# The same kernel with the weights' slots at other addresses: 32 bytes more from slot to slot, and 192 more ahead of the low parts

## The chip, the cores and the metric

One core of a Trainium2 chip. The metric is the device time of one execution in microseconds; the time before is the median of three runs.

## The reference, cut to what matters

Two layers of a hybrid model (latent attention, gated delta rule, block attention side by side) and then four layers of another one, on 256 tokens of 1024 features, all in float32. Most of the arithmetic is the feed-forward block, which the last four layers hold twice each:

```python
def swiglu(x, w_gu, w_down):
    g, u = jnp.split(x @ w_gu, 2, axis=-1)
    return (jax.nn.silu(g) * u) @ w_down
```

with 1024 features in and out and 2816 inside. The other products with weights are projections into and out of the mixers (latent attention, delta rule, linear attentions, windowed attention) and a gate. All of them have the same form in the kernel.

## The kernel before

**Weights as chunks.** The host lays all weights out as 781 chunks of 128 partitions x 1024 float32 (4096 bytes in each partition). Chunk c arrives by DMA in slot c mod 4 of w_raw (load, line 80). ACT writes the high part, a copy rounded to TensorE's fp32r format, into slot c mod 6 of w_hi (hi, line 90). DVE subtracts it from the raw one and writes the low part into slot c mod 6 of w_lo (lo, line 98). The three engines work up to five chunks ahead of TensorE. TensorE reports a chunk as done (chunk_done), and then ACT may fill its slot again.

**Products.** A float32 product is made of three fp32r ones: high weights with high activations (line 138), low weights with high activations (line 139), high weights with low activations (line 144), as products (lines 146 and on) puts them in a row. In each of them 128 columns of a slot are the stationary operand, and 256 columns of activations move. Each matmul is one LDWEIGHTS and one MATMUL, and no two neighbours share both operands. rows (lines 153, 154 and 158) is the same with the roles exchanged: the slot's columns move, 256 or 512 of them, and activations are stationary.

**Order of work.** One feed-forward block (ffn, from line 415 on) takes for each of 22 tiles a gate chunk, an up chunk and the down chunk of the tile before. A gate or up chunk is 8 x 3 products into one half of a bank of ps_gu, the moving operand being xn_hi[:, j, :] and xn_lo[:, j, :], a new j for every three. A down chunk is 8 x 3 products into ps_acc, the moving operand being h_hi[:, t % 2, :] and h_lo[:, t % 2, :], the same for all eight. In the first tile of a block gate and up are made together, and the products alternate between the two halves of the bank. The small projection of p (ple) and the latents of the first two layers lie in h_hi and h_lo too. Every other product with weights moves (or, in rows, holds) xn_hi and xn_lo.

**Where the tensors lie.** setup (lines 722 and on) allocates the tensors one after another, each rounded up to 32 bytes, in every partition alike. By the compiled program of the kernel before they begin at these bytes of a partition:

| tensor | begins at | modulo 512 |
|---|---|---|
| w_raw, 4 slots of 4096 | 16,512 | 128 |
| w_hi, 6 slots of 4096 | 32,896 | 128 |
| w_lo, 6 slots of 4096 | 57,472 | 128 |
| x_res, xn | 82,048 and 90,240 | 128 |
| xn_hi (two), xn_lo (two) | 98,432 to 123,008, steps of 8192 | 128 |
| silu, h | 132,512 and 134,560 | 416 |
| h_hi, h_lo, 4 slices of 1024 each | 136,608 and 140,704 | 416 |
| ones, const | 146,176 and 154,880 | 256 |
| arena | 165,536 | 160 |

Slices of 128 columns in a chunk and the slices of xn and h are multiples of 512 bytes apart.

Of the kernel before, what the change touches and what calls it, by code (L numbers as in the profile page):

```python
# [7 lines left out]
F32R = mybir.dt.float32r  # L8
# [4 lines left out]
P = 128  # L13
# [5 lines left out]
FT = FF // P  # L19
CH = 1024  # L20
NS = 6
NR = 4
TURN = 12
STEP = 4
AHEAD = NS - 1
EPS = 1e-6
# [29 lines left out]
class Kernel:  # L56
# [19 lines left out]
    def load(self, sp, c, i=0):  # L76
        s = c % NR
        if c >= NR:
            sp.wait_ge(self.w_lo_ready.sem, c - NR + 1 + i * TURN)
        sp.dma_start(self.w_raw[:, s, :], self.w_dram[c + i * TURN, :, :]).then_inc(self.w_loaded[s].sem, 16)  # L80

    def hi(self, act, c, i=0):

        if c >= self.n_chunks:
            return
        s, r = c % NS, c % NR
        act.wait_ge(self.w_loaded[r].sem, 16 * (c // NR + 1) + i * 16 * (TURN // NR))
        if c >= NS:
            act.wait_ge(self.chunk_done.sem, c - NS + 1 + i * TURN)
        act.activation(self.w_hi[:, s, :], self.w_raw[:, r, :], ACT.Copy).then_inc(self.w_hi_ready.sem, 1)  # L90

    def lo(self, dve, c, i=0):

        if c >= self.n_chunks:
            return
        s = c % NS
        dve.wait_ge(self.w_hi_ready.sem, c + 1 + i * TURN)
        dve.tensor_tensor(self.w_lo[:, s, :], self.w_raw[:, c % NR, :], self.w_hi[:, s, :], ALU.subtract)\  # L98
           .then_inc(self.w_lo_ready.sem, 1)
# [315 lines left out]
def ffn(k):  # L415
# [27 lines left out]
    def _(pe):  # L443
        def down(t, c, i):
            pe.wait_ge(*hl.at(b0 + t + 1 + STEP * i))
            k.wait_chunk(pe, c, i)
            for m in range(KD):
                mm = k.products(pe, k.ps_acc[:, m // 2, (m % 2) * S:(m % 2 + 1) * S], c % NS, m * P, P,
                                k.h_hi[:, t % 2, :], k.h_lo[:, t % 2, :], False, t == FT - 1,
# [272 lines left out]
def setup(nc, ctx, io, n_chunks, n_vec, n_const=1):  # L722
    k = Kernel(nc, ctx, n_chunks)
    k.w_dram = io["w"]
    k.w_raw = k.sb("w_raw", [P, NR, CH])
    k.w_hi = k.sb("w_hi", [P, NS, CH], F32R)
    k.w_lo = k.sb("w_lo", [P, NS, CH], F32R)
    k.x = k.sb("x_res", [P, KD, S])
    k.xn = k.sb("xn", [P, KD, S])
    k.xh = [k.sb(f"xn_hi{b}", [P, KD, S], F32R) for b in range(2)]  # L730
    k.xl = [k.sb(f"xn_lo{b}", [P, KD, S], F32R) for b in range(2)]
    k.cur, k.read_until, k.p_read = 1, [0, 0], 0
    k.rstd = k.sb("rstd", [P, S])
    k.rcol = k.sb("rstd_columns", [P, TT])
    k.mean_sq = k.sb("mean_square_columns", [P, TT])
    k.powers = k.sb("powers", [P, 2 * TT])
    k.latent_col = k.sb("latent_columns", [P, 2 * TT])
    k.eps = k.sb("eps", [P, TT])
    k.inner_sq, k.inner_col, k.outer_col = (k.sb(n, [P, TT]) for n in ("inner_square_columns", "inner_columns", "outer_columns"))
    k.both_gains = k.sb("both_gains", [P, KD])  # L740
    k.inner = None
    k.norms = 0
    k.s = k.sb("silu", [P, 2, S])
    k.h = k.sb("h", [P, 2, S])
    k.h_hi = k.sb("h_hi", [P, 4, S], F32R)
    k.h_lo = k.sb("h_lo", [P, 4, S], F32R)
    k.lat_hi, k.lat_lo = k.h_hi[:, 0:3, :], k.h_lo[:, 0:3, :]
    k.vec = k.sb("vec", [P, n_vec])
    k.ones = k.sb("ones", [P, P])
    k.p_all = k.sb("p_all", [P, 4, 2, S])  # L750
    k.t5b = k.p_all[:, :, :, :].rearrange("p a b t -> p (a b) t").rearrange("p (q h) t -> p q h t", q=2)
    k.const = k.sb("const", [P, n_const])
    k.t5 = k.sb("t5", [33, 4])
    k.ba = k.sb("ba", [P, 16])
    k.tiny = k.sb("tiny", [P, 16])
    k.lbw = k.sb("bounds", [P, 8 * KD])
    k.arena = Arena(k.sb("arena", [P, ARENA]), ARENA)
    k.acc_by = []
    k.slot = k.side_bank = 0
    k.y_at = {}  # L760
    k.adds = None
    k.late = ((), ())
    ps = [ctx.enter_context(nc.psum_tensor(f"ps_gu{i}", [P, 2 * S], F32)) for i in range(2)]
    k.ps_gu = ps
    k.ps_acc = ctx.enter_context(nc.psum_tensor("ps_acc", [P, 4, 2 * S], F32))
    k.ps_sum = ctx.enter_context(nc.psum_tensor("ps_sum", [P, 2 * S], F32))
    k.ps_misc = ctx.enter_context(nc.psum_tensor("ps_misc", [P, 2 * S], F32))
    k.w_loaded = [k(f"w_loaded{s}") for s in range(NR)]
    k.w_hi_ready, k.w_lo_ready, k.chunk_done = k("w_hi_ready"), k("w_lo_ready"), k("chunk_done")
    k.gu_read = [k("product_read_act").made()] * 2  # L770
    k.side_read = [k("product_read_dve").made()] * 2
    k.block = ctx.enter_context(nc.Block())
    return k
# [3106 lines left out]
def build(nc, io, out, n_chunks):  # L3880
    with ExitStack() as ctx:
        k = setup(nc, ctx, io, n_chunks, N_VEC, N_CONST_1)
        k.ident = con(k, "ident")
        start(k, io)
# [89 lines left out]
```

## Time and profile before

| | |
|---|---|
| median of 3 runs | 2543.4 us (2542.41 to 2544.77) |
| span of the profiled execution | 2542.1 us; the page gives no other time of it |
| PE busy | 2497.2 us |
| DVE busy | 1729.5 us |
| ACT busy | 1322.2 us |
| DMA, mean | 165 GB/s |

The span goes from the first to the last instruction of the profiled execution, and is 1.3 us under the median of the runs. Busy times of PE are of overlapping instructions: a MATMUL of 256 columns is shown with some 285 ns, while the next starts much earlier. The distance from start to start is what one costs. The timeline gives starts to 0.01 us, so a pace is read over many products in a row.

### The profile page before, as it was taken

To read this page: it belongs to the slowest core of one execution; us is meant where nothing else is said; L and a number is where in the kernel's file an instruction comes from. 1 tells how busy PE (TensorE), PEld (TensorE's weight loads), DVE (VectorE), ACT (ScalarE), POOL (GpSimd) and SP (SyncE) were. 2 spreads that over 40 slices of the span, in tenths; PEclk is the share of its full clock that TensorE was granted. 3 is DMA by queue.
4 is the path that set the end of the run, shared out by engine and by line. 5 is a ranking of instruction groups with operands and counts; after the bars stand their busy time and mean duration, and the time that the engine had idled before them with its cause. 6 is when DMAs were issued, how large, how long until landed. Compare 5 with 4: busy or idle time off the path is not lost.

```text
span 2542.1 us, 51688 instructions
## 1 busy us (share of the span) xinstructions
PE 2497.2 (98%) x20402; PEld 2466.2 (97%) x20402; DVE 1729.5 (68%) x2416; ACT 1322.2 (52%) x2021; POOL 97.1 (4%) x99
## 2 busy tenths in 40 slices
PE   8989989999999999999999999999999999999999
PEld 7989989999999999999999999998999999999999
DVE  7768767657775576657666675587666765877556
ACT  5735735446664454445544554466445544755444
POOL 1010010000200000000000000000000000220000
PEclk9999999999999999999999999999999999999999
DMA  7314315554345555555355455543555555435553
GB/s 255 108 51 164 119 51 193 180 189 167 141 156 185 183 179 181 179 187 175 133 191 181 165 192 189 183 141 116 194 185 171 188 179 186 161 122 183 182 184 122
DMA packets 115233, 418.85 MB, mean 165 GB/s; under 512 B 12816, under 2 KB 13968, under 8 KB 114832
## 3 DMA queue, kind: packets, MB, share of 16 engines
q1 hardware_dynamic: 114240, 413.10, 47.2%
q8 instruction: 108, 1.77, 0.3%
q0 software_dynamic: 560, 2.10, 0.2%
q10 hardware_dynamic: 288, 1.57, 0.2%
q14 instruction: 37, 0.30, 0.0%
HBM read 414.62 MB, written 2.10 MB: 164 GB/s over the span
## 4 chain that ended last, share of the span: by engine, by line
PE 88%; DVE 7%; ACT 2%; issue 1%; DMA 0%; POOL 0%; SPq 0%; ACTq 0%; DVEq 0%
PE ps_gu L138 17%; PE ps_gu L144 17%; PE ps_gu L139 17%; PE ps_acc L144 8%; PE ps_acc L138 8%; PE ps_acc L139 8%; DVE w_lo L98 2%; PE ps_acc L2641 1%; DVE arena L1615 1%; ACT w_hi L90 1%; PE ps_acc L2207 1%; PE ps_sum L138 1%; PE ps_sum L366 1%; PE ps_sum L139 1%; PE ps_sum L144 1%
## 5 line engine op out<-in xcount | busy, mean ns | idle before, releaser
L98 DVE TENSOR_TENSOR w_lo<-w_raw,w_hi 128x1024 fp32r<-128x1024 f32 x781 | 953.6, 1226 | 423.2 <-ACT w_hi L90 422.7
L138 PE MATMUL ps_gu<-xn_hi,w_hi 128*128 128x256 f32 x3832 | 1084.2, 286 | 28.4 <-DVE w_lo L98 13.0
L139 PE MATMUL ps_gu<-xn_hi,w_lo 128*128 128x256 f32 x3832 | 1076.2, 284 | 0.0
L144 PE MATMUL ps_gu<-xn_lo,w_hi 128*128 128x256 f32 x3832 | 1035.9, 284 | 0.0
L90 ACT ACTIVATE w_hi<-w_raw 128x1024 fp32r<-128x1024 f32 x781 | 819.7, 1054 | 411.2 <-PE ps_gu L144 303.8
L138 PEld LDWEIGHTS ps_gu<-xn_hi,w_hi 128*128 128x128 f32 x3832 | 738.1, 193 | 33.5 <-DVE w_lo L98 13.7
L139 PEld LDWEIGHTS ps_gu<-xn_hi,w_lo 128*128 128x128 f32 x3832 | 739.0, 193 | 0.2
L144 PEld LDWEIGHTS ps_gu<-xn_lo,w_hi 128*128 128x128 f32 x3832 | 714.9, 192 | 0.0
L144 PE MATMUL ps_acc<-h_lo,w_hi 128*128 128x256 f32 x1496 | 420.4, 281 | 0.0
L138 PE MATMUL ps_acc<-h_hi,w_hi 128*128 128x256 f32 x1496 | 419.6, 280 | 0.2 <-DVE h_lo L545 0.2
L139 PE MATMUL ps_acc<-h_hi,w_lo 128*128 128x256 f32 x1496 | 416.5, 278 | 0.0
L515 ACT ACTIVATE silu<-ps_gu 128x256 f32<-128x256 f32 x176 | 67.9, 386 | 450.9 <-DVE ps_gu L536 450.9
L138 PEld LDWEIGHTS ps_acc<-h_hi,w_hi 128*128 128x128 f32 x1496 | 281.9, 188 | 0.4 <-DVE h_lo L545 0.4
L139 PEld LDWEIGHTS ps_acc<-h_hi,w_lo 128*128 128x128 f32 x1496 | 281.9, 188 | 0.0
L144 PEld LDWEIGHTS ps_acc<-h_lo,w_hi 128*128 128x128 f32 x1496 | 280.7, 188 | 0.0
L536 DVE TENSOR_TENSOR ps_gu<-ps_gu,rstd 128x512 f32<-128x512 f32 x176 | 123.1, 699 | 87.9 <-PE ps_gu L144 87.6
L540 DVE TENSOR_TENSOR h<-silu,ps_gu 128x256 f32<-128x256 f32 x176 | 74.2, 422 | 90.2 <-ACT silu L515 90.2
L138 PE MATMUL ps_acc<-xn_hi,w_hi 128*128 128x256 f32 x336 | 96.3, 290 | 0.3 <-DVE w_lo L98 0.3
L139 PE MATMUL ps_acc<-xn_hi,w_lo 128*128 128x256 f32 x336 | 93.9, 283 | 0.0
L393 POOL TENSOR_TENSOR rstd_columns<-mean_square_columns,powers 128x2 f32<-128x2 f32 x17 | 15.1, 886 | 1978.7 <-ACT mean_square_columns L379 1978.7
L144 PE MATMUL ps_acc<-xn_lo,w_hi 128*128 128x256 f32 x336 | 88.6, 283 | 0.0
L545 DVE TENSOR_TENSOR h_lo<-h,h_hi 128x256 fp32r<-128x256 f32 x176 | 73.9, 420 | 7.7 <-ACT h_hi L519 7.7
(462 smaller groups left out, 2651.3 us busy)
## 6 DMA issues: line engine op xcount, KB each, us to landing
w_raw<-in_w_dram SPq DMA_DIRECT2D x781, 512.0 KB, 3.9
const<-in_const_dram SPq DMA_DIRECT2D x1, 1280.0 KB, 12.2
x_res<-in_x_dram SPq DMA_DIRECT2D x2, 512.0 KB, 7.6
distance_rows<-arena POOLq DMA_DIRECT2D x1, 1024.0 KB, 5.8
p_all<-distance_rows POOLq DMA_DIRECT2D x2, 512.0 KB, 6.0
p_all<-in_p_dram ACTq DMA_DIRECT2D x1, 1024.0 KB, 7.7
out_dram<-x_res SPq DMA_DIRECT2D x8, 128.0 KB, 1.9
const<-in_const_dram ACTq DMA_DIRECT2D x1, 512.0 KB, 9.6
```

The costliest lines, as they stand in the source:

```text
L90: act.activation(self.w_hi[:, s, :], self.w_raw[:, r, :], ACT.Copy).then_inc(self.w_hi_ready.sem, 1)
L98: dve.tensor_tensor(self.w_lo[:, s, :], self.w_raw[:, c % NR, :], self.w_hi[:, s, :], ALU.subtract)\
L138: pe.matmul(out, self.w_hi[:, s, j0:j0 + width], rhs_hi, start=start, stop=False, skip_group_check=True)
L139: pe.matmul(out, self.w_lo[:, s, j0:j0 + width], rhs_hi, start=False, stop=False, skip_group_check=True)
L144: return pe.matmul(out, self.w_hi[:, s, j0:j0 + width], rhs_lo, start=False, stop=last, skip_group_check=True)
L366: mm = pe.matmul(k.ps_sum[:, tt:tt + 1], k.xn[:, m, tt * P:(tt + 1) * P], k.ones[:, 0:1], start=(m == 0 and tt == 0), stop=(m == tiles[-1] ...
L515: act.activation(k.s[:, t % 2, :], k.ps_gu[t % 2][:, 0:S], ACT.Silu).then_inc(silu.sem, 1)
L536: dve.tensor_tensor(gu, gu, k.rstd[:, :].unsqueeze(1).to_broadcast([P, 2, S]), ALU.mult).then_inc(sc.sem, 1)
L540: dve.tensor_tensor(k.h[:, t % 2, :], k.s[:, t % 2, :], k.ps_gu[t % 2][:, S:2 * S], ALU.mult)\
L545: dve.tensor_tensor(k.h_lo[:, t % 2, :], k.h[:, t % 2, :], k.h_hi[:, t % 2, :], ALU.subtract)\
L1615: eng.scalar_tensor_tensor(out=qkv[:, t, :], in0=raw[:, b, j:j + S], scalar=w(j), in1=qkv[:, t, :], op0=ALU.mult, op1=ALU.add).then_inc(*c ...
L2207: mm = pe.matmul(at_bank(acc01, n), four(Lm[lv % 2])[:, n, :], four(T)[:, n, :], start=(n % 4 == 0), stop=True, skip_group_check=True)
```

## The change

The slots of w_hi and of w_lo are made 1032 columns long in place of 1024; the eight columns at the end of each (32 bytes) are not used. Between the two tensors lies an unused one of 48 columns (192 bytes). Every tensor that is allocated after them moves up by 576 bytes. No instruction is added, removed or put elsewhere.

```diff
@@ -19,6 +19,7 @@
 FT = FF // P
 CH = 1024
 NS = 6
+SHIFT = 8
 NR = 4
 TURN = 12
 STEP = 4
@@ -723,8 +724,9 @@
     k = Kernel(nc, ctx, n_chunks)
     k.w_dram = io["w"]
     k.w_raw = k.sb("w_raw", [P, NR, CH])
-    k.w_hi = k.sb("w_hi", [P, NS, CH], F32R)
-    k.w_lo = k.sb("w_lo", [P, NS, CH], F32R)
+    k.w_hi = k.sb("w_hi", [P, NS, CH + SHIFT], F32R)[:, :, 0:CH]
+    k.sb("w_between", [P, 6 * SHIFT])
+    k.w_lo = k.sb("w_lo", [P, NS, CH + SHIFT], F32R)[:, :, 0:CH]
     k.x = k.sb("x_res", [P, KD, S])
     k.xn = k.sb("xn", [P, KD, S])
     k.xh = [k.sb(f"xn_hi{b}", [P, KD, S], F32R) for b in range(2)]
```

## Rows read from the trace of the kernel before

**Rows 1.** The page: span, busy time, granted clock, and the chain that ended last

```profile
span 2542.1 us, 51688 instructions
...
PE 2497.2 (98%) x20402; PEld 2466.2 (97%) x20402; DVE 1729.5 (68%) x2416; ACT 1322.2 (52%) x2021; POOL 97.1 (4%) x99
...
PEclk9999999999999999999999999999999999999999
...
PE 88%; DVE 7%; ACT 2%; issue 1%; DMA 0%; POOL 0%; SPq 0%; ACTq 0%; DVEq 0%
PE ps_gu L138 17%; PE ps_gu L144 17%; PE ps_gu L139 17%; PE ps_acc L144 8%; PE ps_acc L138 8%; PE ps_acc L139 8%; DVE w_lo L98 2%; PE ps_acc L2641 1%; DVE arena L1615 1%; ACT w_hi L90 1%; PE ps_acc L2207 1%; PE ps_sum L138 1%; PE ps_sum L366 1%; PE ps_sum L139 1%; PE ps_sum L144 1%
```

**Rows 2.** Groups by line and shape: products with the weights, first of each three

```profile
L138 PE MATMUL ps_gu<-xn_hi,w_hi 128*128 128x256 f32 x3832 | 1084.2, 286 | 28.4 <-DVE w_lo L98 13.0 <-ACT xn_hi L204 10.4 <-ACT xn_hi L1184 1.3
...
L138 PE MATMUL ps_acc<-h_hi,w_hi 128*128 128x256 f32 x1496 | 419.6, 280 | 0.2 <-DVE h_lo L545 0.2
...
L138 PE MATMUL ps_acc<-xn_hi,w_hi 128*128 128x256 f32 x336 | 96.3, 290 | 0.3 <-DVE w_lo L98 0.3
...
L138 PE MATMUL ps_misc<-xn_hi,w_hi 128*128 128x256 f32 x184 | 53.4, 290 | 0.0
...
L138 PE MATMUL ps_sum<-xn_hi,w_hi 128*128 128x256 f32 x152 | 45.0, 296 | 1.9 <-ACT xn_hi L1184 1.9
```

**Rows 3.** Timeline of PE, 1300 to 1312 us: down, gate and up, down; start us, duration us, instruction

```profile
1305.14 0.28 PE L138 MATMUL ps_gu<-xn_hi,w_hi 128*128 128x256 f32 x1
...
1308.02 0.28 PE L138 MATMUL ps_acc<-h_hi,w_hi 128*128 128x256 f32 x1
...
1308.38 0.28 PE L138 MATMUL ps_acc<-h_hi,w_hi 128*128 128x256 f32 x1
...
1310.85 0.28 PE L138 MATMUL ps_gu<-xn_hi,w_hi 128*128 128x256 f32 x1
...
1311.20 0.28 PE L138 MATMUL ps_gu<-xn_hi,w_hi 128*128 128x256 f32 x1
```

**Rows 4.** Timeline of PE, 51 to 53 us: the roles of weights and h exchanged

```profile
51.38 0.28 PE L1819 MATMUL ps_misc<-w_hi,h_hi 128*128 128x256 f32 x1
...
52.08 0.28 PE L138 MATMUL ps_gu<-xn_hi,w_hi 128*128 128x256 f32 x1
```

**Rows 5.** Chain in order of time: sixteen products in a row; start us, us, what

```profile
1153.22 1.92 PE ps_gu L144 x16
```

**Rows 6.** Timeline of PE: products 512 columns wide, two stretches

```profile
650.49 0.39 PE L154 MATMUL ps_acc<-w_lo,xn_hi 128*128 128x512 f32 x1
...
650.95 0.40 PE L153 MATMUL ps_acc<-w_hi,xn_hi 128*128 128x512 f32 x1
...
652.34 0.39 PE L153 MATMUL ps_acc<-w_hi,xn_hi 128*128 128x512 f32 x1
...
652.79 0.40 PE L158 MATMUL ps_acc<-w_hi,xn_lo 128*128 128x512 f32 x1
...
655.28 0.39 PE L158 MATMUL ps_acc<-w_hi,xn_lo 128*128 128x512 f32 x1
...
657.32 0.39 PE L158 MATMUL ps_acc<-w_hi,xn_lo 128*128 128x512 f32 x1
```

**Rows 7.** Groups by line and shape: the splits of the weights, and two narrower splits

```profile
L98 DVE TENSOR_TENSOR w_lo<-w_raw,w_hi 128x1024 fp32r<-128x1024 f32 x781 | 953.6, 1226 | 423.2 <-ACT w_hi L90 422.7
L90 ACT ACTIVATE w_hi<-w_raw 128x1024 fp32r<-128x1024 f32 x781 | 819.7, 1054 | 411.2 <-PE ps_gu L144 303.8 <-PE ps_acc L144 68.1 <-DMA w_raw<-in_w_dram 17.6
...
L545 DVE TENSOR_TENSOR h_lo<-h,h_hi 128x256 fp32r<-128x256 f32 x176 | 73.9, 420 | 7.7 <-ACT h_hi L519 7.7
L519 ACT ACTIVATE h_hi<-h 128x256 fp32r<-128x256 f32 x176 | 71.7, 407 | 7.8 <-DVE h L540 7.8
```

## The prediction

> **What bounds the kernel now.** I read the page first: the span, the share of each engine, the granted clock, the chain that ended last [rows 1]. The reader is to see that PE is busy 98% of 2542.1 us, that its clock was granted in full in all forty slices, and that 88% of the chain lies on PE, three quarters of the whole on lines 138, 139 and 144, with 2% on DVE's split and 1% on ACT's. So the kernel lasts as long as its matmuls take one after another; engines that prepare weights are ahead of it. The durations in the page (some 285 ns) overlap and are no pace; the pace has to be read from starts.
>
> Second the groups, for counts [rows 2]. Each line that is shown stands for three products (138, 139, 144). Moving operand x: 3 x (3832 + 336 + 184 + 152) = 13,512 products. Moving operand h: 3 x 1496 = 4,488 (176 down chunks of 24, and some for p and the latents, which lie in the same tensors).
>
> Third the timeline, for the pace [rows 3]. A whole gate or up chunk, 24 products on x, takes from 1305.14 to 1308.02: 2.88 us, **120.0 ns** each. In the down chunk behind it the 21 products from 1308.38 to 1310.85 take 2.47 us: **117.6 ns** each. Same shape, clock and lines, 2.4 ns apart. The products 512 columns wide take 226.7 ns at best (655.28 to 657.32, nine of them, 2.04 us) [rows 6]. Twice 120.0 less 226.7 is 13.3 ns: what a product takes beyond its columns, about 11 ns where h moves.
>
> What differs between the two chunks? Not the PSUM target: sixteen products that go to the two halves of a bank in turn still take 1.92 us, 120.0 ns each [rows 5]. Not which operand moves: with h stationary and weights moving, six products take 51.38 to 52.08, 0.70 us, 117 ns [rows 4]. What is left is where the operands begin. In the kernel before, w_hi, w_lo and all four parts of xn begin 128 bytes past a multiple of 512, and slots, columns and j step in multiples of 512; h_hi and h_lo begin 416 past one. 
> **The change part by part.** It adds and removes no instruction, wait or DMA. It moves addresses: slot s of w_hi goes up by 32s bytes; slot s of w_lo by 192 + 192 + 32s = 384 + 32s (24 KiB grow by six times 32 bytes, then 192 bytes between); everything behind w_lo by 576. All else keeps its distance to its neighbours; w_raw stays.
>
> The splits of the weights. DVE reads w_raw and w_hi and writes w_lo, ACT reads w_raw and writes w_hi; before, all three stand alike modulo 512, after, not. DVE takes 1226 ns for 1024 columns and 420 for 256: 1.05 ns a column; ACT 1054 and 407: 0.84 ns [rows 7]. Neither shows a stall that grows with the width, so there is nothing to gain, and I cost it at 0. The bound above: the splits are hidden behind PE, which waited about 13 us for DVE's split in the groups of weight products [rows 2]; those waits lie at the starts of stages. If each DVE split took a tenth longer, those 13 us would grow with it, by 1.3 us; I allow 2. Nothing below 0.
>
> The products on x. Distance x less w_hi becomes 64 - 32s, x less w_lo 192 - 32s. Modulo 64 that is 0 in slots 0, 2 and 4 and 32 in slots 1, 3 and 5. A slot that is 32 off should run as h does now, 120.0 less 117.6 or 117.8. I take the whole down chunk of this trace with its slower first triple, 1308.02 to 1310.85, 2.83 us, so 117.9, for a chunk that has such an edge, and 117.6 inside: 2.2 ns less as a middle. Half of 13,512 times 2.2 ns is **-14.9 us**.
>
> The products on h. Distance to w_hi becomes 352 - 32s, to w_lo 480 - 32s: 32 modulo 64 in slots 0, 2, 4, and 0 in 1, 3, 5. Half of them lose what they have: 2244 times 2.2 ns is **+4.9 us**.
>
> The bounds of these two terms: if only distance 0 of a longer period is bad, all of the x products gain and h keeps what it has, 13,512 x 2.2 = -30 us; if distances in the trace are all that ever help, or the effect isn't one of addresses, 0; and above 0, since other distances may be worse than today's (below). The 288 products of 512 columns add at most 0.6 us. Sum: -14.9 + 4.9 = **-10 us**. The profiled execution's span, 2542.1 us, is 1.3 us under the median of 2543.4; I subtract from the median: **2533 us**.
>
> A rule speaks against all of this. The rows say that two chunks of equal products differ by 2.4 ns each [rows 3]. The Trainium skill, "SBUF — State Buffer", section "SBUF: two separate sides", holds that PE and ACT never wait on anyone at the SBUF's ports, and "TensorE: Matmul & The Clock Gate", section "Step-by-step: what each phase is for", that loading the next weights takes no read bandwidth from the running matmul. By that rule the sum is 0. The trace doesn't agree about a product's pace, as far as I can read it, but shows no cause by itself.
>
> **The rivals.**
>
> *No effect of addresses.* The 117.6 ns come from something else in the down chunks, as the reuse of one slice of h by eight triples. For it: the first triple on x behind a down chunk still takes 0.35 us (1310.85 to 1311.20), 117 ns, though its addresses are those of the slow ones [rows 3]; history plays a part. Against it: rows 4, another loop with the same pace. The sum is 0: 2543 us. This is also the case of the pages' rule. Chance 0.16.
>
> *A longer period.* Only equal distances modulo 256 or 512 are bad; then nearly all x products go to 117.8, and h stays: -30 us, 2513. For it: no row says that 64 is the period. Chance 0.21.
>
> *The other side: a worse lock.* The pace settles into a pattern that depends on how the two reads meet, and some new distances meet worse. Place: x products of three of the six slots. For it: products of 512 columns show it at one and the same distance, 650.49 to 652.79, ten in 2.30 us, 230.0 ns against 226.7 elsewhere [rows 6], 231.7 between 650.95 and 652.34. Price: 6756 products times 3.3 ns = +22 us, 2566. It decides from the point where the mean over all products with weights is more than today's, that is where three slots lose on x more than the other cases gain: at +0.4 ns on all 13,512 x products it is past 5 us. Against it: all other chunks settle into one pattern within a few products. Chance 0.20, spread between 0 and this price.
>
> *Much more.* Some distances remove the whole 13.3 ns. If three slots do so, 6756 x 13.3 = -90 us, 2453. Against it: h, which stands apart by 288, got only 2.4. Chance 0.06.
>
> **How the numbers follow.** Half the slots fast, half as now: 0.37, 2533 us, its own range 2529 to 2539 (a step between 1.5 and 3 ns gives -7 to -14 us; the splits' 2 us on top). No change 0.16; longer period 0.21; worse lock 0.20; much more 0.06. The range takes in the longer period and the lower half of the worse lock: 2510 to 2557; outside are much more and the rest of the worse lock, under 0.2. A measurement of this kernel tells about 0.2% (5 us) from nothing. Faster than that: 0.31 of the first case, 0.21 and 0.06: 0.58. Within: 0.16, 0.06 of the first and 0.04 of the worse lock: 0.26. Slower: 0.16.
>
> **What would show it.** Start to start inside gate and up chunks alternates with the slot: 2.83 us in slots 1, 3, 5 and 2.88 in 0, 2, 4, and down chunks the other way round; counts of instructions, DVE's 1226 ns and ACT's 1054 ns stay. All gate chunks at 2.83: longer period. None: no effect of addresses. Chunks over 2.9 us: the worse lock. The forecast is wrong if the pace goes by slot in any order other than odd and even, or if the splits become slower and PE waits for w_lo inside a stage.

## The result and the profile after

The changed kernel takes **2515.1 us** (median of 3, 2514.56 to 2515.61) against 2543.4 before: a ratio of 0.9889, 95% interval 0.9875 to 0.9903. That is 28.3 us less. I had forecast 10 less, and the price of my rival "a longer period", 30 less, lies next to it.

The page of the changed kernel, the lines that answer to [rows 1]:

```profile
span 2513.1 us, 51688 instructions
...
PE 2463.5 (98%) x20402; PEld 2431.3 (97%) x20402; DVE 1729.1 (69%) x2416; ACT 1323.3 (53%) x2021; POOL 96.7 (4%) x99
...
PEclk9999999999999999999999999999999999999999
...
PE 86%; DVE 9%; ACT 3%; issue 1%; DMA 1%; POOL 0%; SPq 0%; ACTq 0%; DVEq 0%
...
L99 DVE TENSOR_TENSOR w_lo<-w_raw,w_hi 128x1024 fp32r<-128x1024 f32 x781 | 953.4, 1227 | 414.5 <-ACT w_hi L91 411.9
...
L91 ACT ACTIVATE w_hi<-w_raw 128x1024 fp32r<-128x1024 f32 x781 | 821.1, 1056 | 400.0 <-PE ps_gu L145 289.6
```

(Line numbers are one higher than before.) The reader is to see what did not move: the counts, the granted clock, the length of a split on DVE (1227 ns for 1226) and on ACT (1056 for 1054) [rows 7]. PE is still busy 98% of the span. What PE does not cover of the span went from 2542.1 - 2497.2 = 44.9 us to 49.6 us: some 5 us of the gain were given back to waits. The gain is in the pace of products.

Six chunks in a row of the changed kernel, in slots 4, 5, 0, 1, 2 and 3, in the timeline of PE (start us, duration us, instruction; the first product of each chunk and of the seventh):

```profile
1290.64 0.28 PE L139 MATMUL ps_gu<-xn_hi,w_hi 128*128 128x256 f32 x1
...
1293.43 0.28 PE L139 MATMUL ps_acc<-h_hi,w_hi 128*128 128x256 f32 x1
...
1296.19 0.28 PE L139 MATMUL ps_gu<-xn_hi,w_hi 128*128 128x256 f32 x1
...
1298.95 0.28 PE L139 MATMUL ps_gu<-xn_hi,w_hi 128*128 128x256 f32 x1
...
1301.80 0.28 PE L139 MATMUL ps_acc<-h_hi,w_hi 128*128 128x256 f32 x1
...
1304.65 0.28 PE L139 MATMUL ps_gu<-xn_hi,w_hi 128*128 128x256 f32 x1
...
1307.50 0.28 PE L139 MATMUL ps_gu<-xn_hi,w_hi 128*128 128x256 f32 x1
```

Slot 4 (x) takes 2.79 us, slot 5 (h) 2.76, slot 0 (x) 2.76, slot 1 (x) 2.85, slot 2 (h) 2.85, slot 3 (x) 2.85. Before, a chunk on x took 2.88 and one on h 2.83, whatever its slot [rows 3]. It is by slot, then, but not by odd and even, and two kinds of chunk run faster than any did before. The same over the whole trace, the median of start to start of undisturbed chunks of 24 products, in ns, with the distance of the moving operand behind w_hi and w_lo, both modulo 256 bytes:

| slot | x: distances | x: chunk | per product | h: distances | h: chunk | per product |
|---|---|---|---|---|---|---|
| 0 | 64, 192 | 2760 | 115.0 | 96, 224 | 2871 | 119.6 |
| 1 | 32, 160 | 2849 | 118.7 | 64, 192 | 2767 | 115.3 |
| 2 | 0, 128 | 2853 | 118.9 | 32, 160 | 2848 | 118.7 |
| 3 | 224, 96 | 2840 | 118.3 | 0, 128 | 2850 | 118.8 |
| 4 | 192, 64 | 2769 | 115.4 | 224, 96 | 2833 | 118.0 |
| 5 | 160, 32 | 2829 | 117.9 | 192, 64 | 2760 | 115.0 |
| before, all | 0, 0 | 2880 | 120.0 | 32, 32 | 2832 | 118.0 |

(An undisturbed chunk is one in which no two starts in a row are 160 ns or more apart.) Chunks on x and on h that stand at the same distances have the same pace in this kernel, to 0.4 ns, though they lie in other tensors and in other slots. Inside the shortest of them the pace falls to 340 ns for three products, **113.3 ns** each, after some slower ones at the entry.

**Where the 29 us came from.** Mean start to start of all undisturbed products on x (the same count of some 13,250 in both traces): 119.86 ns before, 117.39 after, so 13,512 x 2.47 = -33.4 us. On h: 117.98 and 117.68, so -1.3 us. With +4.7 us of PE's idle time that makes -30; the spans differ by 29.0. What is left lies with the products whose moving operand is a slot's columns. Those of 256 columns went from 119.8 to 117.6 ns (156 of them, -0.3 us), but the 288 of 512 columns became slower, 228.0 to 232.0 ns in the mean, +1.2 us. Two products of 512 columns in the changed kernel, nine starts apart:

```profile
649.94 0.40 PE L159 MATMUL ps_acc<-w_hi,xn_lo 128*128 128x512 f32 x1
...
652.03 0.40 PE L159 MATMUL ps_acc<-w_hi,xn_lo 128*128 128x512 f32 x1
```

That is 2.09 us for nine, 232.2 ns each, where the kernel before had 2.04, 226.7 each [rows 6].

### The profile page after: what moved, and what is told of

The parts are those of the page before. It is cut to its first block, busy times and chain, and to the rows that moved or that the text cites. A ratio compares the mean times of both kernels' runs of the same rounds, so it can differ in the third digit from the quotient of the medians.

```text
span 2513.1 us, 51688 instructions
## 1 busy us (share of the span) xinstructions
PE 2463.5 (98%) x20402; PEld 2431.3 (97%) x20402; DVE 1729.1 (69%) x2416; ACT 1323.3 (53%) x2021; POOL 96.7 (4%) x99
## 4 chain that ended last, share of the span: by engine, by line
PE 86%; DVE 9%; ACT 3%; issue 1%; DMA 1%; POOL 0%; SPq 0%; ACTq 0%; DVEq 0%
PE ps_gu L139 16%; PE ps_gu L145 16%; PE ps_gu L140 16%; PE ps_acc L139 8%; PE ps_acc L145 8%; PE ps_acc L140 8%; DVE w_lo L99 2%; PE ps_acc L2643 1%; DMA w_raw<-in_w_dram 1%; DVE arena L1617 1%; ACT w_hi L91 1%; PE ps_acc L2209 1%; ACT xn_hi L205 1%; PE ps_sum L367 1%; PE ps_sum L139 1%
## 5 line engine op out<-in xcount | busy, mean ns | idle before, releaser
L99 DVE TENSOR_TENSOR w_lo<-w_raw,w_hi 128x1024 fp32r<-128x1024 f32 x781 | 953.4, 1227 | 414.5 <-ACT w_hi L91 411.9
L139 PE MATMUL ps_gu<-xn_hi,w_hi 128*128 128x256 f32 x3832 | 1074.0, 284 | 31.6 <-DVE w_lo L99 13.3
L140 PE MATMUL ps_gu<-xn_hi,w_lo 128*128 128x256 f32 x3832 | 1064.7, 281 | 0.0
L91 ACT ACTIVATE w_hi<-w_raw 128x1024 fp32r<-128x1024 f32 x781 | 821.1, 1056 | 400.0 <-PE ps_gu L145 289.6
L145 PE MATMUL ps_gu<-xn_lo,w_hi 128*128 128x256 f32 x3832 | 1024.6, 281 | 0.0
L139 PEld LDWEIGHTS ps_gu<-xn_hi,w_hi 128*128 128x128 f32 x3832 | 726.7, 190 | 36.8 <-DVE w_lo L99 15.5
L140 PEld LDWEIGHTS ps_gu<-xn_hi,w_lo 128*128 128x128 f32 x3832 | 726.1, 189 | 0.3
L145 PEld LDWEIGHTS ps_gu<-xn_lo,w_hi 128*128 128x128 f32 x3832 | 703.0, 189 | 0.0
```

Source lines behind the costliest of these rows:

```text
L139: pe.matmul(out, self.w_hi[:, s, j0:j0 + width], rhs_hi, start=start, stop=False, skip_group_check=True)
L140: pe.matmul(out, self.w_lo[:, s, j0:j0 + width], rhs_hi, start=False, stop=False, skip_group_check=True)
L145: return pe.matmul(out, self.w_hi[:, s, j0:j0 + width], rhs_lo, start=False, stop=last, skip_group_check=True)
```

## The experiments

All leave the computation as it is and start from the kernel before. They only put unused columns between tensors, so they change distances and nothing else. Distances below are modulo 256 bytes, to w_hi and to w_lo.

**A first map with uniform slots.** No pitch, so all six slots alike. x32, x64 and x96 put 32, 64 or 96 bytes ahead of x_res; both64 puts another 96 bytes ahead of h_hi:

```diff
     k.w_lo = k.sb("w_lo", [P, NS, CH], F32R)
+    k.sb("pad_x", [P, 16])      # x64; 8 columns in x32, 24 in x96
     k.x = k.sb("x_res", [P, KD, S])
...
+    k.sb("pad_h", [P, 24])      # both64 only
     k.h_hi = k.sb("h_hi", [P, 4, S], F32R)
```

> No pitch; everything behind w_lo moved up by 32 bytes, so that in all slots x stands 32 behind the weights and h 320 (64 modulo 256). Theory A (the distance between the two operands decides, period 128, best at 64): x products near 118 ns (as the changed kernel's slot 1), h products 113.3 ns; 2543 - 13512 x 2 - 4488 x 4.4 ns = about 2497 us. Theory B (only a variety of slots helps, a uniform shift does nothing): 2543. My forecast's period of 64: x 117.8, h 120: 2523.

> No pitch; everything behind w_lo moved by 64 bytes: x 64 behind the weights in all slots, h 352 (96 modulo 256). Theory A: all x products at 113.3 ns, h near 119: 2543 - 13512 x 6.6 + 4488 x 1 ns = about 2458 us. Theory B: 2543. A period of 64: x at 120 and h at 117.6 as before, 2543.

> Everything behind w_lo moved by 96 bytes: x 96, h 384 (128 modulo 256, 0 modulo 128). Theory A: x near 118.5 and h, if the period is 128, at 120: about 2533 us; if it is 256, h at some other pace than 120. Theory B: 2543.

> x moved by 64 and h_hi, h_lo and all behind them by 160 (448 behind the weights, 64 modulo 128, 192 modulo 256). Theory A: all products with weights at 113.3 ns: 2543 - 13512 x 6.6 - 4488 x 4.4 ns = about 2434 us, if the engines that feed TensorE keep up. Theory B: 2543. If h needs 64 modulo 256, h stays near 118 and the time near 2455.

Measured: x32 2504.2 us (two runs, 2500.16 and 2508.22; ratio 0.9846 [0.9825, 0.9866]); x64 2529.1 (0.9947 [0.9930, 0.9963]); x96 2549.8 (1.0025 [1.0015, 1.0035]), slower than before; both64 2506.5 (0.9857 [0.9841, 0.9874]).

In x64 (timeline of PE: a chunk on h, one on x, and the start of the next):

```profile
1299.54 0.28 PE L138 MATMUL ps_acc<-h_hi,w_hi 128*128 128x256 f32 x1
...
1302.42 0.28 PE L138 MATMUL ps_gu<-xn_hi,w_hi 128*128 128x256 f32 x1
...
1305.25 0.28 PE L138 MATMUL ps_gu<-xn_hi,w_hi 128*128 128x256 f32 x1
```

The roles are swapped: h, now at 96, takes 2.88 us (120.0 ns), and x at 64 takes 2.83 (117.8). So theory B, that only variety helps, falls, and so does my period of 64 bytes: x at 64 should have stayed at 120. But theory A named the wrong size: x at 64 ran at 117.8, not at the 113.3 ns of slot 0, and 2458 us became 2529. In x96 x at 96 is back at 120.0 (2880 ns) and h at 128 takes 118.8 (2851 ns): a distance of 128 is not one of 0. In x32 x takes 116.7 (2800 ns), though h, at the same 32 and 32, takes 118.0 in the kernel before: equal distances do not always give equal paces from kernel to kernel.

Something new shows in x32 and both64. In both64 theory A expected 2434 us. Of its 591 undisturbed chunks 142 ran within 1% of 2720 ns, and 446 near 2827. Those near 2720 are mostly on h, at 192 (125 of 179, against 17 of 412 on x, at 64), but both paces occur on either operand. In x32 h stands at 64 in all slots, and of its 182 undisturbed chunks 42 ran at 113.3 ns and 139 near 117.9. So at one pair of addresses in one kernel **two paces** can last.

**Controls.** all64 moves every tensor by 64 bytes; raw64 puts 64 bytes between w_raw and w_hi, so that only the operands of DVE's and ACT's splits move against each other; x256 moves x and h by 256 bytes against the weights.

```diff
+    k.sb("pad_all", [P, 16])    # all64
     k.w_raw = k.sb("w_raw", [P, NR, CH])
+    k.sb("pad_raw", [P, 16])    # raw64
     k.w_hi = k.sb("w_hi", [P, NS, CH], F32R)
     k.w_lo = k.sb("w_lo", [P, NS, CH], F32R)
+    k.sb("pad_x", [P, 64])      # x256
     k.x = k.sb("x_res", [P, KD, S])
```

> A control: 64 bytes ahead of w_raw, so every tensor moves by 64 and every distance stays. If distances decide: 2543 us, 2880 ns a gate chunk, 2832 a down chunk. If where an operand begins by itself decides: as the kernel with x moved by 64, or another time.

> 64 bytes between w_raw and w_hi: the operands that DVE and ACT read and write stand 64 apart instead of 0, TensorE's own stand as before. If only TensorE's two operands matter: 2543 us, 2880 ns and 2832 ns a chunk. If the splits' accesses take part in TensorE's pace: other paces.

> Everything behind w_lo moved by 256 bytes: distances of x 256, of h 544. If the period is 256 bytes: 2543 us, 2880 ns a gate chunk and 2832 a down chunk, as before. If it is 512 or more: other paces.

Measured: 2543.4 us (0.9999 [0.9989, 1.0009]), 2543.7 (1.0002 [0.9991, 1.0012]) and 2544.1 (1.0001 [0.9991, 1.0012]), each with 2880 ns for a chunk on x and 2832 or 2833 for one on h. So moving everything by 64 bytes does not matter, nor do the distances between the splits' operands as far as 64 bytes show, and a distance of 256 bytes is as good as none: the period is 256 bytes or a part of it. It is not 128: with that period h in x96 (at 128 and 128) and x in slot 2 of the changed kernel (at 0 and 128) should run at the 120.0 ns of x in the kernel before, and they take 118.8 and 118.9.

**The 192 bytes and the two parts.** pitch is the change without the 192 bytes; lo64 moves w_lo alone by 64 bytes against all else:

```diff
-    k.w_hi = k.sb("w_hi", [P, NS, CH], F32R)
-    k.w_lo = k.sb("w_lo", [P, NS, CH], F32R)
+    k.w_hi = k.sb("w_hi", [P, NS, CH + 8], F32R)[:, :, 0:CH]    # pitch
+    k.w_lo = k.sb("w_lo", [P, NS, CH + 8], F32R)[:, :, 0:CH]
...
     k.w_hi = k.sb("w_hi", [P, NS, CH], F32R)                    # lo64
+    k.sb("pad_mid", [P, 16])
     k.w_lo = k.sb("w_lo", [P, NS, CH], F32R)
+    k.sb("pad_x", [P, 112])
     k.x = k.sb("x_res", [P, KD, S])
```

> The change without the 192 bytes between: pitch of 32 bytes alone. x less w_hi is 128 - 32s (modulo 256), x less w_lo 192 - 32s as in the changed kernel. Theory C: no slot has 64 and 192, so no chunk runs at 113.3 ns; mean near 118.5, about 2525 us. Theory D: the slots with one distance at 64 (2, 4 and 0) run in part at 113.3: nearer 2510. If the 192 bytes do nothing: 2515 as the changed kernel.

> w_lo alone moved by 64 against w_hi, x (0 to w_hi) and h (288 to w_hi) as before. If the pace comes from the reads of the next product's stationary operand beside this product's moving one, only the product before each w_lo changes, and the three of a triple differ: at most a third of what the kernel with x at 64 gained on x (120.0 to 117.7), -0.8 ns on 13512: about 2532 us. If it comes from the distance of the high parts alone: 2543.

pitch: 2519.5 us (0.9902 [0.9885, 0.9918]). No chunk runs at 113.3 ns; the best, slot 2 on x at 64 and 128 and slot 3 on h at the same, take 2788 to 2791 and 2787 ns, 116.2 ns. So the pitch alone brings 24 us. The 192 bytes seem to bring 4 more: the intervals of the two ratios overlap, but in the traces the mean over x is 117.88 ns here and 117.39 with them. Their unlike paces again agree where distances agree.

lo64: 2521.7 us (two runs; 0.9913 [0.9893, 0.9933]), 10 us under what I expected. x, at 0 behind w_hi as before and 192 behind w_lo, takes 117.8 ns (2827 a chunk), in all three products of a triple and not only before each w_lo (its inner triples read 118, 118, 118, 117, 119, 117). Moving one of the two parts changes the pace of all: a product is not priced by its own pair of operands alone.

**Is the fast pace the distances' own?** slot0 gives all slots the distances of the changed kernel's slot 0. best takes 64 and 192 for x and 192 and 64 for h, the two fast pairs:

```diff
     k.w_hi = k.sb("w_hi", [P, NS, CH], F32R)
+    k.sb("pad_mid", [P, 96])    # slot0; 32 columns in best
     k.w_lo = k.sb("w_lo", [P, NS, CH], F32R)
+    k.sb("pad_x", [P, 48])      # both
...
+    k.sb("pad_h", [P, 24])      # best only
     k.h_hi = k.sb("h_hi", [P, 4, S], F32R)
```

> The distances of the changed kernel's slot 0 in all slots, no pitch: x 64 behind w_hi and 192 behind w_lo, h 96 and 224. Theory C: x 113.3 ns, h 119.7 (as slot 0 of the changed kernel): 2543 - 13512 x 6.6 + 4488 x 1.7 ns = about 2462 us. Theory D: x 117.7, h 120: about 2529, as with x at 64 alone.

> No pitch. w_lo 128 bytes further from w_hi, x 64 behind w_hi and 192 behind w_lo (modulo 256), h 192 behind w_hi and 64 behind w_lo: the pairs of the changed kernel's chunks that ran at 113.3 ns, now in all slots. Theory C (a pair of distances 64 and 192, so hi and lo 128 apart, makes 113.3 ns the only pace that lasts): all products at 113.3 ns, about 2434 us plus what the feeding engines add. Theory D (hi and lo apart makes no difference; at 64 the pace is 117.7 or 113.3 by how a stretch is entered): as the kernel with x and h at 64 alone, 2506.

slot0, timeline of PE: two chunks on x, and the start of one on h.

```profile
1301.13 0.28 PE L138 MATMUL ps_gu<-xn_hi,w_hi 128*128 128x256 f32 x1
...
1303.88 0.28 PE L138 MATMUL ps_gu<-xn_hi,w_hi 128*128 128x256 f32 x1
...
1306.60 0.28 PE L138 MATMUL ps_acc<-h_hi,w_hi 128*128 128x256 f32 x1
```

best, the same view: a chunk on h, one on x, and the start of the next.

```profile
1303.99 0.28 PE L138 MATMUL ps_acc<-h_hi,w_hi 128*128 128x256 f32 x1
...
1306.71 0.28 PE L138 MATMUL ps_gu<-xn_hi,w_hi 128*128 128x256 f32 x1
...
1309.56 0.28 PE L138 MATMUL ps_gu<-xn_hi,w_hi 128*128 128x256 f32 x1
```

In both kernels x stands 64 and 192 behind the weights. In slot0 a chunk on x that follows one on h takes 2.75 us, and the next, with no entry to make, 2.72 (2720 ns, 113.3 each). In best it takes 2.85, 118.7 ns, through the chunk. The two kernels also differ in the distance from w_hi to w_lo (384 and 128), but best alone shows both paces: of its chunks on x that follow another on x, 42 took 2720 ns and 191 took 2840 or more. So theory C is refuted: the same operands at the same distances last at 113.3 or at 118.7 ns. Times: slot0 2489.3 and 2510.7 us in its two runs (median 2500.0, ratio 0.9826; the interval, 0.9776 to 0.9876, is wide for that reason; its trace is of the faster one), best 2504.0 (0.9842 [0.9826, 0.9858]). Theory D's 2506 came for best, but its 2529 for slot0 did not, nor its 2510 for pitch.

**Keeping the pace.** If a pace is entered and then lasts, x and h should stand alike, so that nothing changes between chunks. same64 puts both at 64 and 192, same192 both at 192 and 64, same64flat both at 64 and 64:

```diff
     k.w_hi = k.sb("w_hi", [P, NS, CH], F32R)
+    k.sb("pad_mid", [P, 32])    # none in same64flat
     k.w_lo = k.sb("w_lo", [P, NS, CH], F32R)
+    k.sb("pad_x", [P, 16])      # same192 and same64flat; 48 columns in same64
     k.x = k.sb("x_res", [P, KD, S])
...
+    k.sb("pad_h", [P, 56])
     k.h_hi = k.sb("h_hi", [P, 4, S], F32R)
```

> w_lo 128 further; x and h alike: 64 behind w_hi and 192 behind w_lo (modulo 256). Theory E (at these distances two paces last, 113.3 and 118.7 ns; which one holds is set where a stretch is entered, and a chunk that keeps the distances keeps the pace): x and h chunks of one block all at 2720 ns once 113.3 is reached: about 2434 us plus some 10 of waits, 2445; if the other pace is entered, all near 118.7 and 2520. Theory C (the distances alone fix 113.3): 2445 as well, but it has lost already on x after h in the last call.

> The mirror image: x and h both 192 behind w_hi and 64 behind w_lo. Theory E: again one pace through a block, 113.3 or 118.7 ns; by the h chunks of the last call, which reached 113.3 in these distances from x at 118.7, it is 113.3: about 2445 us.

> x and h both 64 behind w_hi and 64 behind w_lo; no extra distance between w_hi and w_lo. If the 128 bytes between the parts are needed to hold 113.3 ns: chunks at 2827 ns (117.8) or a mixture, 2500 to 2510 us. If only the sameness of x and h matters: 2720 ns a chunk and about 2458 us as with x and h at 64 and 192.

same192, the page's first line and the timeline of PE (chunks on h, x, x, and the start of one on h):

```profile
span 2456.4 us, 51688 instructions
```

```profile
1300.69 0.28 PE L138 MATMUL ps_acc<-h_hi,w_hi 128*128 128x256 f32 x1
...
1303.41 0.28 PE L138 MATMUL ps_gu<-xn_hi,w_hi 128*128 128x256 f32 x1
...
1306.13 0.28 PE L138 MATMUL ps_gu<-xn_hi,w_hi 128*128 128x256 f32 x1
...
1308.85 0.28 PE L138 MATMUL ps_acc<-h_hi,w_hi 128*128 128x256 f32 x1
```

Every chunk of the stretch takes 2.72 us, 113.3 ns a product. Over the trace 578 of 586 undisturbed chunks do, to 1%. The time is **2456.4 us** (four runs, 2454.35 to 2458.36; ratio 0.9654 [0.9638, 0.9670]): 87 us under the kernel before and 59 under the changed one. The sum from the paces, 2543 - 13,512 x (119.86 - 113.69) - 4488 x (117.97 - 113.45) ns = 2543 - 83 - 20, gives 2440. PE's idle time, 57.4 us of the span for 44.9 before, accounts for 12.5 us of the rest; in the first products of gate and up chunks it went from 28.4 [rows 2] to 36.0. Some 4 us are not accounted for.

same64: 2460.8 us (2460.13 to 2470.26; 0.9686 [0.9666, 0.9707]), 550 of 591 chunks fast. Its timeline of PE, a chunk on h, one on x behind it, and the start of the next:

```profile
1302.49 0.28 PE L138 MATMUL ps_acc<-h_hi,w_hi 128*128 128x256 f32 x1
...
1305.21 0.28 PE L138 MATMUL ps_gu<-xn_hi,w_hi 128*128 128x256 f32 x1
...
1307.93 0.28 PE L138 MATMUL ps_gu<-xn_hi,w_hi 128*128 128x256 f32 x1
```

This is the cleanest pair of all: same64 and best differ only in the padding ahead of h_hi. All that a product on x reads lies at the same addresses in both, and still a chunk on x takes 2.72 us here and 2.85 in best (376 of 414 fast here, 50 of 413 there). What differs is where h_hi and all behind it lie, and so where the products on h between them read. So what came before a chunk has a part in its pace; the runs show no more of how.

same64flat: 2478.0 (2475.53 to 2491.26; 0.9758 [0.9727, 0.9789]), between the two expected times: 387 chunks near 2720 ns and 200 near 2827, whole stretches of each. So the 128 bytes between high and low parts are not needed for the fast pace, but with them it is taken up far more often.

## Why the prediction was wrong

**What bounds the kernel: right.** PE's pace moved the time, less some 5 us of added waits; counts, clock and splits stayed as told.

**The reading that distance decides: right as far as it went.** The runs that only move operands apart (x64, x32), with the three controls at 2543 or 2544 us, settle it against "no effect of addresses". The doubt that I noted for that rival, the first triple on x behind a down chunk at 117 ns [rows 3] (118.0 in the mean over the trace), was a true sign of something I did not follow up: history decides too, between two paces at one distance (same64 against best).

**The step that failed** is "A slot that is 32 off should run as h does now", which took the effect as one of 64 bytes, with two levels. The period is 256 bytes, the distances to w_hi and to w_lo both count, and there are more than two paces: 113.3, 116.2, 116.7, 117.8, 118.7 and 120.0 ns have all been seen to last. No slot of x was left at 120.0: instead of half the slots at -2.2 ns and half at 0 the mean over x was -2.47 (the term of -14.9 us measured -33.4). And h did not lose +4.9: slots 1 and 5 reached 113.3 ns inside, slot 0 lost 1.6 ns and slots 2 and 3 some 0.7, the mean was -0.3 ns (-1.3 us). The 288 products of 512 columns, put at 0.6 us at most, lost 1.2.

**The rival "a longer period"** gave 2513 and was right in the period's being longer and in the size, by luck in the second: it had all x products at 117.8 and h unchanged. Two fast slots of six (4.6 and 5.0 ns) and four slots with only 1.1 to 2.1 ns make up the same sum.

**"Much more"** named the excess over the columns, 13.3 ns, as what could go. In the fast slots half of it went, 120.0 to 113.3. The 13.3 ns came from taking the excess as a fixed amount in products of both widths. That does not hold from layout to layout: in same192 the same sum, 2 x 113.7 less 230.4 ns, is below zero. Its objection, that h at 288 had gained only 2.4, was worth nothing, since 288 is just one of the distances. **"A worse lock"**: x96 was slower than before by 0.25%, 3.6 of its 6.2 us by h at 118.8 for 118.0 ns and 1.7 by the products of 512 columns, so the side is real, though small; nothing worse than 120.0 has lasted for whole chunks of products on x. Its evidence, the 512 columns of [rows 6], was a sign too: these products were best as they lay, 228.0 ns in the mean before and 227.9 to 228.1 in the controls, and took 230.4 to 234.0 in every other layout tried.

**The term at 0 for the splits** was right (1227 and 1056 ns). What was missing is that a faster PE gives some 5 us back at waits.

**The rule of the pages.** The runs show the pace of equal products going from 120.0 to 113.3 ns when nothing but addresses changes. The prediction had worked out a sum of 0 from two statements: the Trainium skill, "SBUF — State Buffer", section "SBUF: two separate sides", by which PE never waits at these ports, and "TensorE: Matmul & The Clock Gate", section "Step-by-step: what each phase is for", by which loading the next weights takes no read bandwidth from the running matmul. That sum did not come, and the measurements decide. Whether a port waited or bandwidth was taken no trace shows, so the runs refute what was concluded from the two statements, not each statement by itself.

**What stays open.** That it is the read of the next stationary operand that meets the read of the moving one was my picture of it. The runs show that distances between weights and moving operands matter and that 64 bytes between those of the splits don't; they do not show the reads. Accesses of DVE, ACT and POOL are not the cause of the 120.0: in the kernel before, 974 products on x ran while all three were idle, at 120.0 ns, and 8138 with at least one of them at work throughout, at 119.9; the 1957 beside which no DMA packet was under way took 119.9 too. lo64, where one part's distance changes every product's pace, says that a picture by single pairs is too simple. What selects between two paces at the entry of a stretch is open as well; slot0's two runs, 21 us apart, suggest that it can differ from one execution to the next.

## What to carry to other kernels

Where fp32r matmuls run back to back and each has its own stationary operand, read the pace from start to start and compare groups of equal shape; if they differ by a few per cent, look at the distance between moving and stationary operands modulo 256 bytes, and try it with one padding tensor before anything else. A uniform layout with both moving tensors at the same good distance was worth three times what different distances slot by slot were (87 us against 28); 578 of its 586 chunks kept the fast pace. Look at every width and at both roles: what makes products of 256 columns faster made those of 512 slower here. Price such a change from a run, not from one other distance in the trace.

## What was not expected of the hardware

- The same fp32r products, 128 x 128 by 256 columns, at the full clock and with no wait, last at 113.3 or at 118.7 ns at the same addresses: x in same64 and in best, where only h's addresses differ.
- The layout in which products of 256 columns on x were slowest (120.0 ns) is the one in which products of 512 columns were fastest (226.7 ns at best).
- 64 bytes between w_hi and w_lo, with x and h where they were against w_hi modulo 512, take 22 us off the kernel.
- Nothing came under 113.3 ns. The Trainium skill, "TensorE: Matmul & The Clock Gate", section "Wait — 56ns, not 53.3ns?", has N / 2.4 GHz + 2.5 ns, which would be 109.2 ns here as an estimate; no run here reached it with these products.
